# First attention of a two-block transformer: softmax weights divided by their sums on VectorE before they are turned, values as the stationary operand, outputs kept with channels on partitions

## The reference

```python
qh, kh, vh = heads(q), heads(k), heads(v)          # 8 heads of 64 channels, 512 tokens
outs = [_dilated_branch(qh, kh, vh, w, d) for (w, d) in DILATED_BRANCHES]
m_all = jnp.maximum(jnp.maximum(outs[0][0], outs[1][0]), outs[2][0])
num = sum(jnp.exp(m - m_all)[..., None] * acc for (m, l, acc) in outs)
den = sum(jnp.exp(m - m_all) * l for (m, l, acc) in outs)
o = num / den[..., None]
...
attn = _rms_norm(_dilated_attention(q, k, v), attn_out_gain[i])   # mean of squares over 512 channels
rw = _rwkv7(r_r, k_r, v_r, xw, xa, xg, ...)
mixed = jnp.concatenate([attn, rw], axis=-1) @ w_out[i]
```

## Time and profile before

| | |
|---|---|
| time, median of 3 runs | 1293.64 us (1290.81 to 1295.12) |
| profiled execution: its own time | 1293.62 us |
| profiled execution: span, first to last instruction | 1291.9 us |
| granted TensorE clock, mean | 0.992 of full |
| busy: TensorE matmuls, weight loads | 1248.2 us, 1147.6 us |
| busy: VectorE, ScalarE, GpSimd | 759.6 us, 582.2 us, 404.7 us |
| the interleaved stage | about 184 to 342 us of the span |

### The profile page before, as it was taken

How to read it: one execution, slowest core, us unless ns; L and a number is a source line. 1 busy time by engine, 2 the same in 40 slices (tenths; PEclk the granted TensorE clock), 3 DMA queues, 4 the chain that set the end, 5 groups by cost and what they waited for, 6 DMA issues and landing times.

```text
span 1291.9 us, 26564 instructions
## 1 busy us (share of the span) xinstructions
PE 1248.2 (97%) x11253; PEld 1147.6 (89%) x11253; DVE 759.6 (59%) x1028; ACT 582.2 (45%) x1026; POOL 404.7 (31%) x314
## 2 busy tenths in 40 slices
PE   7999989999899999999999999999999999999997
PEld 7677787888799899999999997776798999999997
DVE  5579735455348726739558467434575395583763
ACT  5445525445335525526336353545444163361552
POOL 8022235233102525336235224000042362352520
PEclk9999989999899999999999999999999999999999
DMA  6223300000252232324332423210232233333331
GB/s 211 66 65 98 98 1 3 3 3 3 99 164 66 99 98 81 116 66 130 101 98 89 141 74 98 66 66 33 82 98 98 66 122 108 98 99 98 99 115 66
DMA packets 102073, 109.40 MB, mean 85 GB/s; under 512 B 1970, under 2 KB 97252, under 8 KB 101956
## 3 DMA queue, kind: packets, MB, share of 16 engines
q1 hardware_dynamic: 101876, 107.45, 26.3%
q0 software_dynamic: 80, 0.26, 0.1%
HBM read 105.60 MB, written 2.10 MB: 83 GB/s over the span
## 4 chain that ended last, share of the span: by engine, by line
PE 87%; DVE 6%; ACT 3%; DVEq 1%; issue 1%; POOL 0%; DMA 0%; ACTq 0%
PE ps L534 11%; PE ps L535 11%; PE ps L536 11%; PE ps L625 6%; PE ps L626 6%; PE ps L627 6%; PE ps L499 4%; PE ps L501 4%; PE ps L500 4%; PE ps L585 1%; DVE w_lo L1812 1%; PE ps L587 1%; PE ps L586 1%; ACT w_hi L1220 1%; PE ps L815 1%
## 5 line engine op out<-in xcount | busy, mean ns | idle before, releaser
L534 PE MATMUL ps<-w_hi,a_hi 128*128 128x256 f32 x1024 | 286.0, 279 | 0.0
L535 PE MATMUL ps<-w_lo,a_hi 128*128 128x256 f32 x1024 | 285.8, 279 | 0.0
L536 PE MATMUL ps<-w_hi,a_lo 128*128 128x256 f32 x1024 | 285.8, 279 | 0.0
L535 PEld LDWEIGHTS ps<-w_lo,a_hi 128*128 128x128 f32 x1024 | 192.4, 188 | 0.1
L534 PEld LDWEIGHTS ps<-w_hi,a_hi 128*128 128x128 f32 x1024 | 192.4, 188 | 0.1
L536 PEld LDWEIGHTS ps<-w_hi,a_lo 128*128 128x128 f32 x1024 | 192.4, 188 | 0.0
L1812 DVE TENSOR_TENSOR w_lo<-w_raw,w_hi 128x2048 fp32r<-128x2048 f32 (+1 forms) x57 | 136.8, 2400 | 85.6 <-ACT w_hi L1220 85.3
L1220 ACT ACTIVATE w_hi<-w_raw 128x2048 fp32r<-128x2048 f32 (+1 forms) x57 | 108.2, 1898 | 132.2 <-PE ps L536 107.5
L2690 POOL TENSOR_TENSOR hsq<-tmp 128x512 f32<-128x512 f32 x64 | 96.0, 1516 | 90.0 <-ACT tmp L1332 62.2
L1918 DVE TENSOR_TENSOR w_lo<-w_raw,w_hi 128x1024 fp32r<-128x1024 f32 (+1 forms) x72 | 95.1, 1335 | 26.5 <-ACT w_hi L1293 26.3
L625 PE MATMUL ps<-th,w_hi 128*128 128x256 f32 x384 | 108.1, 281 | 0.4 <-ACT tmp L1318 0.4
(11 more groups left out here) (379 smaller groups left out, 3104.7 us busy)
## 6 DMA issues: line engine op xcount, KB each, us to landing
w_raw<-w_ffn_up_dram SPq DMA_DIRECT2D x16, 1024.0 KB, 5.6
w_raw<-w_ffn_down_dram SPq DMA_DIRECT2D x16, 1024.0 KB, 5.1
w_raw<-w_up_dram SPq DMA_DIRECT2D x16, 1024.0 KB, 5.7
w_raw<-w_down_dram SPq DMA_DIRECT2D x16, 1024.0 KB, 5.2
w_raw<-w_in_first_dram SPq DMA_DIRECT2D x12, 1024.0 KB, 5.3
w_raw<-w_out_dram SPq DMA_DIRECT2D x8, 1024.0 KB, 5.1
xn<-x_dram SPq DMA_DIRECT2D x8, 512.0 KB, 5.7
w_raw<-w_in_dram SPq DMA_DIRECT2D x4, 1024.0 KB, 5.5
```

The lines of the kernel that those rows point to most:

```text
L534: mm(o, hi[:, hb + k, tok], whi, start=first and own and k == ks[0], stop=False, skip_group_check=True)
L535: mm(o, hi[:, hb + k, tok], wlo, start=False, stop=False, skip_group_check=True)
L536: m = mm(o, lo[:, hb + k, tok], whi, start=False, stop=last and k == ks[-1], skip_group_check=True)
```

## The change

The row sums are applied to the weights instead of to the outputs. VectorE takes the reciprocal of one row sum and multiplies that head's weights in `Z1` (`scaled1(m + 1)`, ahead of `biased(m + 2)`), and `turn_weights` waits for it. `values` runs once for a pair of heads, in the even half steps, ahead of `turn_weights`: values are stationary (64 columns, one head in each column half of the array) and the turned weights of 128 tokens move, so the outputs come with channels on partitions. ScalarE squares each pair of heads' outputs and copies them with the gain (`pair_output`). The sum of squares over channels becomes three matmuls with a matrix of ones (`mix_sum`, at m = 33), the square root and the reciprocal are taken of 512 columns, and the outputs are multiplied by them in m = 37 and 38. `On1`, `mix_norm`, `turn_mix` and `turned_mix` go. `h_hi` is made in m = 38 and 39 and `h_lo` in m = 39. SyncE waits for `p_turned` instead of `o_turned`.

```diff
-            rinv1 = r("rinv1", [P, H])
-            osq1 = r("osq1", [P, H])
-            r("w_hi_rest", [P, 2 * KT * GW - 2 * S - 10 * H])
-            On1 = r("On1", [P, TT, 512])
+            rinv1 = r("rinv1", [P, 4 * H])
+            r("w_hi_rest", [P, 2 * KT * GW - 2 * S - 12 * H])
+            PT1_odd = r("PT1_odd", [P, 2, S])
+            osq1 = r("osq1", [P, 2, S])
...
                             gains()
             load(G_OUT1, a["w_out"][0][:, 0:GW])
-            sp.wait_ge(sm["o_turned"], HP)
+            sp.wait_ge(sm["p_turned"], 4 * H)
             for c in range(1, 3):
                 load(G_OUT1 + c, a["w_out"][0][:, cols_of(c)])
             sp.wait_ge(sm["wu_done"], NB)
...
             def turn_weights(m):
                 n, e = m // 2, m % 2
-                pe.wait_ge(sm["p_ready"], m + 1)
+                pe.wait_ge(sm["w_scaled"], m + 1)
                 after("pt_ready", m)
                 for j in range(n % TT + 1):
                     k = nc.tensor.transpose(ps[:, 6, j * P:(j + 1) * P], Z1[:, n % 2, e, j * P:(j + 1) * P], ident[:, :])
                 k.then_inc(sm["p_turned"], 1)
-            def values(m):
...
+            def values(n):
+                p, t = n // TT, n % TT
+                if t == 0:
                     after("o1_ready", p)
-                pe.wait_ge(sm["pt_ready"], m + 1)
+                pe.wait_ge(sm["pt_ready"], 2 * n + 2)
                 for j in range(t + 1):
-                    k = mm(ps[:, 7, e * 256 + t * N:e * 256 + (t + 1) * N], PT1[:, m % 2, j * P:(j + 1) * P],
-                           Vn[:, j, p * P + e * N:p * P + (e + 1) * N], start=j == 0, stop=j == t)
+                    for e in range(2):
+                        k = mm(ps[half[e], 7, t * P:(t + 1) * P], Vn[:, j, p * P + e * N:p * P + (e + 1) * N],
+                               (PT1, PT1_odd)[n % 2][:, e, j * P:(j + 1) * P], start=j == 0, stop=j == t)
                 k.then_inc(sm["pv_done"], 1)
-            def turn_mix(c):
...
+            def mix_sum():
+                pe.wait_ge(sm["max_ready"], 4 * H)
+                pe.wait_ge(sm["o_added"], 1)
+                pe.wait_ge(sm["o1_ready"], HP)
+                for c, x in enumerate((osq1[:, 0, :], osq1[:, 1, :], PT1[:, 0, :])):
+                    k = mm(ps[:, 4, :], ones[:, :], x, start=c == 0, stop=c == 2)
+                k.then_inc(sm["o_sum"], 1)
             def attend(m):
+                if m and m % 2 == 0 and m <= 4 * H:
+                    values(m // 2 - 1)
                 if m < 4 * H:
                     turn_weights(m)
-                if 0 < m <= 4 * H:
-                    values(m - 1)
-                if 35 <= m < 37:
-                    turn_mix(2 * (m - 35))
-                    turn_mix(2 * (m - 35) + 1)
+                if m == 33:
+                    mix_sum()
...
             def turned_weights(m):
-                w = (m // 2 % TT + 1) * P
+                n = m // 2
+                w = (n % TT + 1) * P
                 act.wait_ge(sm["p_turned"], m + 1)
-                if m > 1:
-                    act.wait_ge(sm["pv_done"], m - 1)
-                af(PT1[:, m % 2, 0:w], ps[:, 6, 0:w], ACT.Copy).then_inc(sm["pt_ready"], 1)
...
+                if n > 1:
+                    act.wait_ge(sm["pv_done"], n - 1)
+                af((PT1, PT1_odd)[n % 2][:, m % 2, 0:w], ps[:, 6, 0:w], ACT.Copy).then_inc(sm["pt_ready"], 1)
+            def pair_output(p):
+                act.wait_ge(sm["pv_done"], TT * (p + 1))
+                if p == 2:
+                    act.wait_ge(sm["o_added"], 1)
+                af((osq1[:, 0, :], osq1[:, 1, :], osq1[:, 1, :], PT1[:, 0, :])[p], ps[:, 7, :], ACT.Square)
+                af(qkT[:, p, :], ps[:, 7, :], ACT.Copy, scale=cols("attn_out_gain", p)).then_inc(sm["o1_ready"], 1)
+            def upper_mix(c):
+                act.wait_ge(sm["o_scaled"], c + 1)
+                act.wait_ge(sm["y_done"], NB - 1)
+                af(h_hi[:, c, :], qkT[:, c, :], ACT.Copy).then_inc(sm["hhi_ready"], 1)
             def attend(m):
...
                     turned_weights(m)
                 if m + 2 < 4 * H:
                     weights(m + 2)
...
+                if m and m % 8 == 0 and m <= 4 * H:
+                    pair_output(m // 8 - 1)
+                if m == 34:
+                    act.wait_ge(sm["o_sum"], 1)
+                    af(PT1_odd[:, 0, :], ps[:, 4, :], ACT.Sqrt, bias=eps[:, 0:1], scale=1.0 / 512).then_inc(sm["o_sd"], 1)
+                if m in (38, 39):
+                    upper_mix(2 * (m - 38))
+                    upper_mix(2 * (m - 38) + 1)
...
-            def pair_output(p):
...
+            def scaled1(m):
+                n, e = m // 2, m % 2
+                w = (n % TT + 1) * P
+                dve.wait_ge(sm["p_ready"], m + 1)
+                v.reciprocal(rinv1[:, m:m + 1], rowsum1[:, m:m + 1])
                 dve.drain()
-                v.tensor_tensor(On1[:, :, p * P:(p + 1) * P].rearrange("q t (e n) -> q e t n", e=2),
-                                ps[:, 7, :].rearrange("q (e t n) -> q e t n", e=2, n=N),
-                                rinv1[:, :].rearrange("q (e t) -> q e t", e=2).unsqueeze(3).broadcast_to([P, 2, TT, N]), ALU.mult)\
-                    .then_inc(sm["o1_ready"], 1)
+                v.tensor_scalar(Z1[:, n % 2, e, 0:w], Z1[:, n % 2, e, 0:w], rinv1[:, m:m + 1], None, ALU.mult)\
+                    .then_inc(sm["w_scaled"], 1)
             def attend(m):
+                if m + 1 < 4 * H:
+                    scaled1(m + 1)
                 if m + 2 < 4 * H:
                     biased(m + 2)
-                if m and m % 8 == 0 and m <= 4 * H:
-                    pair_output(m // 8 - 1)
-                if m == 34:
+                if m == 20:
+                    dve.wait_ge(sm["o1_ready"], 2)
+                    v.tensor_tensor(osq1[:, 0, :], osq1[:, 0, :], osq1[:, 1, :], ALU.add).then_inc(sm["o_added"], 1)
+                if m in (35, 36):
                     dve.wait_ge(sm["o_sd"], 1)
-                    v.reciprocal(osq1[:, 0:TT], osq1[:, 0:TT])
+                    columns = slice((m - 35) * 2 * P, (m - 34) * 2 * P)
+                    v.reciprocal(PT1_odd[:, 0, columns], PT1_odd[:, 0, columns])
+                if m in (37, 38):
                     dve.drain()
-                    for t in range(TT):
-                        v.tensor_scalar(On1[:, t, :], On1[:, t, :], osq1[:, t:t + 1], None, ALU.mult).then_inc(sm["o_scaled"], 1)
-                if m == 38:
+                    for c in range(2 * (m - 37), 2 * (m - 36)):
+                        v.tensor_tensor(qkT[:, c, :], qkT[:, c, :], PT1_odd[:, 0, :], ALU.mult).then_inc(sm["o_scaled"], 1)
+                if m == 39:
                     for c in range(HP):
                         lower(H_OUT1, c, qkT[:, c, :])
+            scaled1(0)
```

More of the change, by code:

```diff
@@ L1091, in values2 @@
                     if 0 < p < 3:
[L1092 removed]
+                        pe.wait_ge(sm["mix_f32"], p)
                     if p == 3:
@@ L1599, in weights @@
                 w = (n % TT + 1) * P
-                at_ = m // 8 * 8 + e * TT + n % TT
                 act.wait_ge(sm["max_ready"], m + 1)
                 af(Z1[:, n % 2, e, 0:w], Z1[:, n % 2, e, 0:w], ACT.Exp, bias=negmax1[:, m:m + 1], scale=-1.0,
-                   accum_out=rowsum1[:, at_:at_ + 1]).then_inc(sm["p_ready"], 1)
+                   accum_out=rowsum1[:, m:m + 1]).then_inc(sm["p_ready"], 1)
             def turned_weights(m):
-                w = (m // 2 % TT + 1) * P
+                n = m // 2
+                w = (n % TT + 1) * P
                 act.wait_ge(sm["p_turned"], m + 1)
-                if m > 1:
-                    act.wait_ge(sm["pv_done"], m - 1)
-                af(PT1[:, m % 2, 0:w], ps[:, 6, 0:w], ACT.Copy).then_inc(sm["pt_ready"], 1)
[L1613 to L1625, removed]
+                if n > 1:
[11 more added lines that the diff above has]
+                af(h_hi[:, c, :], qkT[:, c, :], ACT.Copy).then_inc(sm["hhi_ready"], 1)
             def attend(m):
@@ L1632, in attend @@
                     weights(m + 2)
-                if m == 33:
-                    mix_norm()
-                if 35 <= m < 37:
-                    turned_mix(2 * (m - 35))
-                    turned_mix(2 * (m - 35) + 1)
-                if m == 37:
-                    act.drain()
-                    act.wait_ge(sm["y_done"], NB - 1)
-                    for c in range(HP):
-                        af(h_hi[:, c, :], qkT[:, c, :], ACT.Copy).then_inc(sm["hhi_ready"], 1)
+                if m and m % 8 == 0 and m <= 4 * H:
[6 more added lines that the diff above has]
+                    upper_mix(2 * (m - 38) + 1)
             def beside(i, n):
@@ L2255, in biased @@
                     .then_inc(sm["max_ready"], 1)
-            def pair_output(p):
-                dve.wait_ge(sm["pv_done"], 8 * p + 8)
-                v.reciprocal(rinv1[:, :], rowsum1[:, 8 * p:8 * p + 8])
+            def scaled1(m):
```

(26 more changed lines are left out.)

16 lines of the change are left out of this document (4 added, 12 removed).

## The result

The changed kernel takes 1307.23 us (median of 5 runs, 1302.58 to 1309.38), the kernel before 1293.64 (5 runs): a ratio of 1.0108, 95% interval 1.0087 to 1.0129. The forecast was 1299.1 with a range of 1291 to 1303. The direction was right, the size was not: 13.6 us lost where 5.5 were forecast, outside the range. The profiled execution took 1307.23 us with a span of 1305.5.

What follows compares the result with a forecast made beforehand. The interleaved stage was taken as bound by a loop between TensorE and VectorE, not TensorE's work alone. Levels and last values 5.2 us, norm 0.35, together 5.5 on 1293.62, gave 1299.1 us, range 1291 to 1303.

Steps and rivals of the forecast that it cites:

- VectorE, scaling the weights: First attention: reciprocal and scaling cost 0.44 us for 128 columns to 0.64 for 512; 32 of them 17.2 us.
- `double(2)` waited 1.40 us for GpSimd, whose time doesn't move: back to 0: Levels 0 to 2: the wait at `double(2)` absorbs the early delay of +0.46 and +0.20 us.
- The clock: Third rival, chance 0.12: ScalarE's bank 7 reads block elsewhere, or idle time lowers TensorE's clock; 1302 us.
- ScalarE's pair output: Level 4, end of block 0: square and copy (0.63 + 0.68 us) precede `turn_keys`' copies; delay goes from 1.1 to 2.2.
- the norm: Around m = 33 to 39: transposes removed, three ones matmuls (2.6 us), reciprocals and multiplications added; net +0.35 us.
- the place: Odd half steps: scaling stands ahead of `biased`, on the way to `scores`, and costs; even ones lie beside TensorE.
- about ten levels rather than four, some 10 us rather than 2.5: Expected sign: TensorE's `scores` wait for VectorE's `negmax` at more levels and for longer.
- the values on TensorE: First attention: a pair of heads costs 0.37 to 1.02 us, no column-half overlap; 5.0 us less over four pairs.
- The rival of a further 4.3 us: Fourth rival, chance 0.04: column halves overlap, values cost 4.3 us less, half lost in waits; 1296.9 us.
- only the parts at levels 5, 7, 10 and 15 come through: Of TensorE's 5.0 us saved on values, these levels' parts count; at nine others the scaling is paid.
- The scaling costs only where TensorE waits already: First rival, chance 0.19: only levels 6, 8, 12 and 13 pay, the rest give 4.4 us; 1292.5 us.
- TensorE's work decides: Second rival, chance 0.12: added time stays in VectorE's idle 50%, TensorE's savings on values and norm count; 1288.4 us.

Runs made afterwards that it cites:

- experiment 1: Changed kernel with the scaling given a second operation (add 0.0) and an accumulated output that nobody reads, same place: 1300.63 us, ratio 1.0066.
- experiment 5: Changed kernel with the plain scaling on only the first two columns of each block, same place: 1311.5 us, ratio 1.0159.
- experiment 6: Changed kernel with the scaling on only two columns and in the accumulating form, same place: 1298.04 us, ratio 1.0069.
- experiment 11: Changed kernel with the scaling as a TENSOR_TENSOR of the weights and the broadcast reciprocal, same place: 1313.19 us, ratio 1.0135.
- experiment 2: Changed kernel with the plain scaling moved behind `biased` in both half steps: 1294.85 us, ratio 1.0021.
- experiment 3: Changed kernel without reciprocal and scaling, the transposes waiting for the exponential itself: 1295.74 us, ratio 1.0019.
- experiment 4: Kernel before with the 32 reciprocals and scalings added in the change's place, old values, outputs' division and norm kept: 1309.99 us, ratio 1.0133.
- experiment 8: Changed kernel with the scaling behind `biased` and in the accumulating form: 1293.56 us, ratio 1.0013.
- experiment 10: Changed kernel with the plain scaling behind `biased` in the odd half steps only: 1295.08 us, ratio 1.0021.
- experiment 9: Changed kernel with accumulating scaling behind `biased`, `values` moved to odd half steps and `pair_output` one half step later: 1289.82 us, ratio 0.9980.

## Why the prediction was wrong

**The step that failed** is "VectorE, scaling the weights ... 0.44 for 128 columns, 0.64 for 512 ... 32 of them are 17.2 us". These prices were read in the second attention, where no GpSimd instruction ran beside them (GpSimd was busy 0.00 of the 100 us from 800 to 900). In the first attention GpSimd works on the recurrence, and a scaling that meets it waits for its end. The seven long ones that stood ahead of `biased` after level 0 are 0.16, 0.17, 0.60, 0.99, 0.60, 0.99 and 0.99 us above their undisturbed time, 4.5 us in all, of which 4.2 fall on the five levels at which `scores` then waited (6, 8, 11, 12 and 13). Experiments 1, 5, 6 and 11 show the wait, and show that it hangs on the form of the instruction. The Trainium skill has the rule ("SBUF - State Buffer", "Who interferes with whom"): a plain `tensor_scalar` from SBUF to SBUF can use a port pair that it shares with GpSimd, an instruction with two SBUF inputs uses it too when GpSimd reads SBUF, and of the two engines the second to start is fully blocked; the form that writes out its accumulator stays off it. All three agree with the runs (1.41 and 1.63 us at most against 0.75). A row's price holds only beside the same neighbours.

**A second step failed beside it**, worth some 0.9 us: "`double(2)` waited 1.40 us for GpSimd, whose time doesn't move: back to 0". GpSimd's time moved. It makes the mask after two steps on `xn`, which ScalarE copies behind the delayed exponential (at 200.77 us, before at 199.78), and TensorE waited 1.72 us for it.

**The clock** was a rival at 0.12, and it came on top of the forecast in place of beside it. A run's time goes with its mean clock: the kernel before took 1287.5 to 1290.2 us at 0.997 and 0.998, and 1293.1 to 1295.1 at 0.989, and within the runs of each kernel, taken together, it is 0.7 us for 0.001. The changed kernel's five runs have 0.9856 on the mean, those of the kernel before 0.9919 (the 23 beside experiments 1 to 4): some 4.5 us. The trace gives the same by another way: the three stretches in the levels cost some 1.4 us each, 0.4 us for each us at half clock, as does the long one of experiment 5. A stretch elsewhere can cost less: the changed kernel's profiled execution also had half clock from 11 to 21 us, and its first `scores` are only 0.26 us late. So, as an estimate: 5.5 forecast, 4.5 of waits for GpSimd, 4.5 of clock, 14.5 us, against 14.6 between the means (1306.88 and 1292.28). That it closes so well is in part luck, since terms of the 5.5 were wrong both ways: the mask (0.9 us more), ScalarE's pair output (0.7 less) and the norm (0.5 less). The kernels that wait much (1, 4, 5, 6, 11, the change) have the low mean clocks, 0.981 to 0.989; the others have 0.990 to 0.992. That waiting makes the clock fall is argued from this alone: no run took the falls away by themselves, and not each long wait is followed by one. In the change, waits of 2.48 us that ended at 244.27 and 309.23 were not (TensorE was busy only 1.80 us in the window from 240 to 244, at clock 1.00).

**Right: the place.** The odd half steps pay, the even ones don't. Experiment 8 against 1 prices it at 0.53% (6.9 us) with the clean form, experiment 10 shows that the even half steps are free, and at levels 3, 5, 7 and 10 the steps came within 0.1 us of the forecast. The waits for `negmax` were to be at "about ten levels rather than four, some 10 us rather than 2.5": they are 12.1 us at eight. The nearness of the two sums is in part luck, as 4.2 us of the 12.1 are waits for GpSimd.

**Right in size, wrong in the reading: the values on TensorE.** They take 0.37 and 1.02 us a pair, as forecast. But the prediction says of the two heads' column halves that the rows "show no such overlap: the step is (1.02 - 0.37) / 12 = 0.054 us for each record". The step is a mean over records that start in twos. A narrow window of the timeline shows the two heads' last records together, 0.28 us for both, when one alone lasts 0.273:

```profile
256.32 0.28 PE L946 MATMUL ps<-PT_odd,Vn 128*64 128x128 f32 x2
```

All sixteen records of this pair of heads start in twos, at most 7 ns apart, and from one two to the next it is 0.11 us. That is what one full-width record of 128 columns takes: a quarter of the 0.43 us for 512 (an estimate from the earlier trace rows). So the column halves do run at the same time, and the 0.054 us already holds it. With that the trace agrees with what the prediction cites from the Trainium skill ("TensorE: Matmul & The Clock Gate", "Part 3: Packing small matmuls"). The rival of a further 4.3 us counted it twice.

The forecast also said of the 5.0 us saved that "only the parts at levels 5, 7, 10 and 15 come through". Even that was generous: in experiment 8 nothing comes through (the delay against before changes by +0.19 us from level 0 to level 13). The work was taken from half steps in which VectorE is late; experiment 9 puts work back there and gets 3 to 4 us.

**Off: ScalarE's pair output at level 4.** Forecast +1.1 for the step, measured +0.45, and 0.19 in experiment 8.

**Off, small: the norm.** The matmuls with ones took 2.81 us for a forecast 2.6. From the start of `double(16)` to that of the last `solve` the stage took 27.8 us, before 28.0: -0.2 where +0.35 was forecast. "The stage's delay appears after m = 32" did not come about.

**The rivals.** "The scaling costs only where TensorE waits already" (1292.5 us) falls with the result itself: `scores` waits at eight places in place of four, and experiment 4, with the scaling alone, loses 1.33%. "TensorE's work decides" (1288.4 us) falls with experiment 3, in which 5 us less of TensorE's work gained nothing. The third rival named the clock and a stretch of half speed, but priced it at 3 us and left the forecast's own 5.5 as they were.

## What to carry to other kernels

Before pricing a VectorE instruction by a row, look at what GpSimd does beside that row and what it will do beside the new place; if they meet, choose a form that doesn't wait (or another engine), or put it where VectorE has idle time. An instruction that another engine doesn't need yet goes behind the one that it waits for: here two calls exchanged were worth 11 to 12 us. Work taken from an engine helps only in the half steps where that engine is the late one, and work can be moved into its waits.

## What was not expected of the hardware

- A TENSOR_SCALAR of two columns took 1.22 us beside GpSimd, and 0.23 alone. The wait ends with GpSimd's instruction, and all columns follow: +0.02 to 0.03 us for 2 columns, 0.15 for 256, 0.28 for 512.
- The accumulating form waits for nothing: 214 to 216 ns for two columns in 32 instances, 747 at most for 512; undisturbed, the plain form takes 0.49 for 512. `biased` (one input from SBUF, one from PSUM) doesn't wait either. In the changed kernel it took 0.68 us for 512 columns in the middle of a GpSimd instruction, and 0.68 at 279.43 with none beside it:

```profile
273.80 1.17 POOL L2595 TENSOR_TENSOR ktb<-krkv,dC 128x512 f32<-128x512 f32 x1
```

```profile
273.98 0.68 DVE L2250 CUSTOM_DVE_ANT_0 Z<-lncount,ps 128x512 f32<-128x512 f32 x1
```

- A stretch of half clock of 14 us in the middle of the levels (experiment 5, from 241.24 us). TensorE had been busy for 1.85 of the 4 us before it; the changed kernel, with 1.80 us in the window from 240 to 244, kept the full clock.
